# An expert's pass that holds 96 token rows in place of 128, in a decoder step with a mixture of experts

## The reference, cut to what matters

```python
logits = h @ w_router + b_router              # (288, 8)
top_p, top_e = top_k(softmax(logits), 2)      # two experts of eight for each token
top_p = top_p / sum(top_p)
# assignments sorted by expert, each expert sees only its own tokens
y_e = (silu(x_e @ w_gate[e]) * (x_e @ w_up[e])) @ w_down[e]   # 1024 -> 3584 -> 1024
out[token] += top_p * y_e[slot of the token]
```

## Time and profile before

| | |
|---|---|
| median of three runs | 1741.95 us |
| profiled execution: its own time | 1747.82 us |
| its span | 1746.0 us |
| PE busy, share of the span | 1704.5 us, 98% |
| DVE, ACT busy | 78%, 60% |
| expert stage on PE (first L2350 at 742.8, last at 1730.5) | about 988 us |

### The profile page before, as it was taken

The page is one execution under the profiler, slowest core; times in us unless marked ns, Lnnn a source line. Parts: engine busy times, 40 slices in busy tenths (PEclk is TensorE's granted clock), DMA queues, the critical chain, the costliest instruction groups (busy, mean ns, idle before and its releaser), DMA issues.

```text
span 1746.0 us, 25370 instructions
## 1 busy us (share of the span) xinstructions
PE 1704.5 (98%) x9394; PEld 1430.4 (82%) x9394; DVE 1364.7 (78%) x1601; ACT 1042.8 (60%) x1006; POOL 98.1 (6%) x118
## 2 busy tenths in 40 slices
PE   6999999999999999799999999999999999999998
PEld 3878978999988698588888888888888888888886
DVE  2799474554459964888898998998988988989998
ACT  3345424443344533467777777777777777777776
POOL 0112110000021130200000000000000000000000
PEclk8999998999999999999999999999999999999999
DMA  9885047444457601589999999999999999999997
GB/s 383 326 315 193 26 176 282 158 162 168 169 197 283 215 25 55 203 327 343 350 378 350 360 363 343 373 354 347 358 355 352 364 351 351 375 345 366 361 367 271
DMA packets 73385, 499.49 MB, mean 286 GB/s; under 512 B 8096, under 2 KB 8224, under 8 KB 15296
## 3 DMA queue, kind: packets, MB, share of 16 engines
q1 hardware_dynamic: 69728, 481.17, 72.8%
q0 software_dynamic: 3552, 16.87, 2.5%
HBM read 485.96 MB, written 12.05 MB: 285 GB/s over the span
## 4 chain that ended last, share of the span: by engine, by line
PE 90%; DVE 7%; DMA 1%; issue 1%; ACT 1%; SPq 0%; DVEq 0%; ACTq 0%
PE ps L2350 17%; PE ps L2352 17%; PE ps L2351 17%; PE ps L1789 5%; PE ps L1791 5%; PE ps L1790 5%; PE ps L2149 4%; PE ps L1978 3%; DVE yc L1193 2%; PE ps L1800 2%; PE ps L2327 1%; DMA raw<-units 1%; PE ps L1886 1%; PE ps L1901 1%; PE ps L1899 1%; PE ps L2294 1%
## 5 line engine op out<-in xcount | busy, mean ns | idle before, releaser
L1117 DVE TENSOR_TENSOR wlo<-raw,whi 128x2048 fp32r<-128x2048 f32 x382 | 872.8, 2293 | 174.5 <-ACT whi L721 173.5
L721 ACT ACTIVATE whi<-raw 128x2048 fp32r<-128x2048 f32 x384 | 736.5, 1918 | 257.9 <-PE ps L2352 206.5
L2350 PE MATMUL ps<-whi,ht_hi 128*128 128x512 f32 x896 | 355.8, 397 | 3.2 <-DVE ht_lo L1679 3.2
L2351 PE MATMUL ps<-wlo,ht_hi 128*128 128x512 f32 x896 | 350.0, 391 | 0.0
L2352 PE MATMUL ps<-whi,ht_lo 128*128 128x512 f32 x896 | 349.9, 391 | 0.0
L2350 PEld LDWEIGHTS ps<-whi,ht_hi 128*128 128x128 f32 x896 | 168.6, 188 | 36.4 <-issue 3.5
L2352 PEld LDWEIGHTS ps<-whi,ht_lo 128*128 128x128 f32 x896 | 168.6, 188 | 36.0
L2351 PEld LDWEIGHTS ps<-wlo,ht_hi 128*128 128x128 f32 x896 | 168.9, 188 | 31.7
L2350 PE MATMUL ps<-whi,at_hi 128*128 128x512 f32 x448 | 175.2, 391 | 0.0
L2352 PE MATMUL ps<-whi,at_lo 128*128 128x512 f32 x448 | 174.4, 389 | 0.0
L2351 PE MATMUL ps<-wlo,at_hi 128*128 128x512 f32 x448 | 174.4, 389 | 0.0
(11 more groups left out here) (357 smaller groups left out, 2003.8 us busy)
## 6 DMA issues: line engine op xcount, KB each, us to landing
raw<-units SPq DMA_DIRECT2D x447, 1024.0 KB, 6.1
raw<-units SPq DMA_DIRECT2D x16, 512.0 KB, 5.8
sst<-gdn_in POOLq DMA_DIRECT2D x8, 512.0 KB, 6.0
gdns_out<-sst POOLq DMA_DIRECT2D x8, 512.0 KB, 4.1
qst_out<-qpad POOLq DMA_DIRECT2D x2, 1890.0 KB, 10.8
cst_out<-cpad POOLq DMA_DIRECT2D x2, 1116.0 KB, 12.9
x<-x_in SPq DMA_DIRECT2D x1, 1152.0 KB, 9.2
y_out<-hf SPq DMA_DIRECT2D x2, 576.0 KB, 2.9
```

The costliest lines, as they stand in the source:

```text
L721: act.activation(whi[s % NSPLIT][:, :], raw[u % NRAW][:, :], ACT.Copy).then_inc(hi_split, 1)
L1117: dve.tensor_tensor(wlo[s % NSPLIT][:, :], raw[unit_of(s) % NRAW][:, :], whi[s % NSPLIT][:, :].bitcast(F32), ALU.subtract).then_inc(lo_spl ...
L2350: mm(ps[:, bank, :], a_hi[:, a], whi[u % NSPLIT][:, w], start=(first and i == 0), stop=False)
L2351: mm(ps[:, bank, :], a_hi[:, a], wlo[u % NSPLIT][:, w], start=False, stop=False)
```

## The change

The constant SLOTS = 96 takes the place of 128 in the experts' part. Stationary operands are 96 columns wide (their storage still steps by 128, so that the columns used of a 512-column tile are four pieces of 96). Results have 96 partitions. The four transposes of a group have an identity of 96x96 as moving operand in place of 128x128, and 96 rows of the stationary one. The rounding and the rest behind a transpose (`at_hi`, `at_lo`, `ht_hi`, `ht_lo`) run on 4x96 columns in place of 512; the others (`sge`, `ae`, `xe`, `ye_hi`, `ye_lo`) keep their columns and lose partitions. The scatter contracts over 96 rows. The passes are counted by 96 and 192 in place of 128 and 256. Sizes and positions of all tiles in memory stay, and so do the weights, their transfers, and the splitting of weights into `whi` and `wlo`.

```diff
+SLOTS = 96
+def slots(rows, half=0):
+    return rows[:, half * 512:(half + 1) * 512].rearrange("p (i n) -> p i n", n=P)[:, :, 0:SLOTS]
...
-                    act.activation(ht_hi[q][:, (part - 2) * 512:(part - 1) * 512], ps[:, bank, :], ACT.Copy).then_inc(hthi_ready, 1)
+                    act.activation(slots(ht_hi[q], part - 2), slots(ps[:, bank, :]), ACT.Copy).then_inc(hthi_ready, 1)
...
-                            act.activation(at_hi[c % 2][:, :], ps[:, 4, :], ACT.Copy).then_inc(eahi_ready, 1)
+                            act.activation(slots(at_hi[c % 2]), slots(ps[:, 4, :]), ACT.Copy).then_inc(eahi_ready, 1)
...
-            step(dve.tensor_scalar(npf2[:, 0:1], npf[:, 0:1], 128.5, 1.0, ALU.is_gt, ALU.add))
-            step(dve.scalar_tensor_tensor(npf[:, 0:1], npf[:, 0:1], 256.5, npf2[:, 0:1], ALU.is_gt, ALU.add))
+            step(dve.tensor_scalar(npf2[:, 0:1], npf[:, 0:1], SLOTS + 0.5, 1.0, ALU.is_gt, ALU.add))
+            step(dve.scalar_tensor_tensor(npf[:, 0:1], npf[:, 0:1], 2 * SLOTS + 0.5, npf2[:, 0:1], ALU.is_gt, ALU.add))
...
-                            dve.tensor_tensor(at_lo[c % 2][:, :], ps[:, 4, :], at_hi[c % 2][:, :].bitcast(F32), ALU.subtract)\
+                            dve.tensor_tensor(slots(at_lo[c % 2]), slots(ps[:, 4, :]), slots(at_hi[c % 2]).bitcast(F32), ALU.subtract)\
...
-                                dve.tensor_tensor(ae[c % 2][:, :], ps[:, 2 + c % 2, :], sge[c % 2][:, :], ALU.mult)\
+                                dve.tensor_tensor(ae[c % 2][0:SLOTS, :], ps[0:SLOTS, 2 + c % 2, :], sge[c % 2][0:SLOTS, :], ALU.mult)\
...
-                        last = pe.transpose(ps[:, bank, d * P:(d + 1) * P], xe[:, c:c + P], cc("ident"))
+                        last = pe.transpose(ps[:, bank, d * P:d * P + SLOTS], xe[0:SLOTS, c:c + P], cc("ident", SLOTS, SLOTS))
...
-                mm(ps[:, bank, 0:T], ye_hi[:, w], pt_sel[q][:, :], start=True, stop=False)
+                mm(ps[:, bank, 0:T], ye_hi[0:SLOTS, w], pt_sel[q][0:SLOTS, :], start=True, stop=False)
...
-                                last = pe.transpose(ps[:, 4, i * P:(i + 1) * P], ae[c % 2][:, i * P:(i + 1) * P], cc("ident"))
+                                last = pe.transpose(ps[:, 4, i * P:i * P + SLOTS], ae[c % 2][0:SLOTS, i * P:(i + 1) * P], cc("ident", SLOTS, SLOTS))
...
-                                a = slice((off + i) * P, (off + i + 1) * P)
+                                a = slice((off + i) * P, (off + i) * P + SLOTS)
                                 w = slice(i * 512, (i + 1) * 512)
-                                mm(ps[:, bank, :], a_hi[:, a], whi[u % NSPLIT][:, w], start=(first and i == 0), stop=False)
-                                mm(ps[:, bank, :], a_hi[:, a], wlo[u % NSPLIT][:, w], start=False, stop=False)
-                                last = mm(ps[:, bank, :], a_lo[:, a], whi[u % NSPLIT][:, w], start=False, stop=(end and i == 3))
+                                mm(ps[0:SLOTS, bank, :], a_hi[:, a], whi[u % NSPLIT][:, w], start=(first and i == 0), stop=False)
+                                mm(ps[0:SLOTS, bank, :], a_hi[:, a], wlo[u % NSPLIT][:, w], start=False, stop=False)
+                                last = mm(ps[0:SLOTS, bank, :], a_lo[:, a], whi[u % NSPLIT][:, w], start=False, stop=(end and i == 3))
```

More of the change, by code:

```diff
@@ L1065, in gather @@
                     act.wait_ge(gx_done, g * 2 + part + 1)
-                    act.activation(xe[:, part * 512:(part + 1) * 512], ps[:, bank, :], ACT.Copy).then_inc(gx_copied, 1)
+                    act.activation(xe[0:SLOTS, part * 512:(part + 1) * 512], ps[0:SLOTS, bank, :], ACT.Copy).then_inc(gx_copied, 1)
                 elif part < 4:
                     act.wait_ge(gt_done, g * 2 + part - 1)
-                    act.activation(ht_hi[q][:, (part - 2) * 512:(part - 1) * 512], ps[:, bank, :], ACT.Copy).then_inc(hthi_ready, 1)
+                    act.activation(slots(ht_hi[q], part - 2), slots(ps[:, bank, :]), ACT.Copy).then_inc(hthi_ready, 1)
             def output_high(it, q, a):
@@ L1074, in output_high @@
                 act.wait_ge(unit_used, later(S_MOE + PER_EXPERT - 1 + a, it, PER_EXPERT))
-                act.activation(ye_hi[:, a * 512:(a + 1) * 512], ps[:, 5 + a, :], ACT.Copy, scale=pslot[q])\
+                act.activation(ye_hi[0:SLOTS, a * 512:(a + 1) * 512], ps[0:SLOTS, 5 + a, :], ACT.Copy, scale=pslot[q][0:SLOTS])\
                     .then_inc(yhi_ready, 1)
@@ L1098, in _ @@
                                     act.wait_ge(eg_prod, it * FC + c - 1)
-                                act.activation(sge[c % 2][:, :], ps[:, c % 2, :], ACT.Silu).then_inc(eg_gate, 1)
+                                act.activation(sge[c % 2][0:SLOTS, :], ps[0:SLOTS, c % 2, :], ACT.Silu).then_inc(eg_gate, 1)
                                 if c:
@@ L1676, in gather @@
                 if 2 <= part < 4:
-                    cols = slice((part - 2) * 512, (part - 1) * 512)
                     dve.wait_ge(hthi_ready, g * 2 + part - 1)
-                    dve.tensor_tensor(ht_lo[q][:, cols], ps[:, bank, :], ht_hi[q][:, cols].bitcast(F32), ALU.subtract)\
+                    dve.tensor_tensor(slots(ht_lo[q], part - 2), slots(ps[:, bank, :]), slots(ht_hi[q], part - 2).bitcast(F32), ALU.subtract)\
                         .then_inc(htlo_ready, 1)
@@ L1698, in output_low @@
                 dve.wait_ge(yhi_ready, it * 2 + a + 1)
-                dve.scalar_tensor_tensor(ye_lo[:, a * 512:(a + 1) * 512], ps[:, 5 + a, :], pslot[q],
-                                         ye_hi[:, a * 512:(a + 1) * 512].bitcast(F32),
+                dve.scalar_tensor_tensor(ye_lo[0:SLOTS, a * 512:(a + 1) * 512], ps[0:SLOTS, 5 + a, :], pslot[q][0:SLOTS],
+                                         ye_hi[0:SLOTS, a * 512:(a + 1) * 512].bitcast(F32),
                                          ALU.mult, ALU.subtract).then_inc(ylo_ready, 1)
             def next_pass(p_):
-                dve.tensor_scalar(posm, posm, -128.0, None, ALU.add)
-                dve.tensor_scalar(posT[0:NE, :], posT[0:NE, :], -128.0, None, ALU.add).then_inc(pass_step, 1)
+                dve.tensor_scalar(posm, posm, -float(SLOTS), None, ALU.add)
+                dve.tensor_scalar(posT[0:NE, :], posT[0:NE, :], -float(SLOTS), None, ALU.add).then_inc(pass_step, 1)
                 dve.wait_ge(pass_step, p_ + 1)
@@ L2293, in gather @@
                             pe.wait_ge(tok_lo_ready, i - 1)
-                        last = mm(ps[:, bank, :], pe_sel[:, b * P:(b + 1) * P],
+                        last = mm(ps[0:SLOTS, bank, :], pe_sel[:, b * P:b * P + SLOTS],
                                   tok[:, b * D + part * 512:b * D + (part + 1) * 512], start=(i == 0), stop=(i == 4))
@@ L2311, in scatter @@
                 w = slice(d * P, (d + 1) * P)
-                mm(ps[:, bank, 0:T], ye_hi[:, w], pt_sel[q][:, :], start=True, stop=False)
-                mm(ps[:, bank, 0:T], ye_lo[:, w], pt_sel[q][:, :], start=False, stop=True).then_inc(scat_done, 1)
+                mm(ps[:, bank, 0:T], ye_hi[0:SLOTS, w], pt_sel[q][0:SLOTS, :], start=True, stop=False)
+                mm(ps[:, bank, 0:T], ye_lo[0:SLOTS, w], pt_sel[q][0:SLOTS, :], start=False, stop=True).then_inc(scat_done, 1)
             with pe.Fori(0, n_pass) as p_:
```

## The result

The changed kernel takes 1751.62 us (median of 20 runs, 1744.42 to 1756.56), the one before 1747.31 us (median of 20 runs taken beside them, 1741.62 to 1751.66). The ratio is 1.0027, interval 1.0015 to 1.0038: some 4.7 us slower (4.3 by the medians). I had forecast 1734.5, within 1720 to 1744, and 7.5 us of gain. The first three runs of before lay low by this measure (1741.95); with 1747.31 in its place the forecast would have been 1739.8. So of the 17.1 us between forecast and result 5.4 come from the reference point, and 11.8 from what I said of the change.

What follows compares the result with a forecast made beforehand. PE's matmul steps were taken to bound the experts' stage. Transposes -7.2 us and the first expert's wait -0.3, expert matmuls 0, made -7.5 from 1741.95: 1734.5 us, range 1720 to 1744.

Steps and rivals of the forecast that it cites:

- What bounds the kernel: Experts' stage: PE, never idle, sets the pace by number of matmuls times step; DMA at most 0.97, nothing late next.
- The transposes: 288 transposes on PE's path, 128 to 96 moving columns: 0.112 to 0.084-0.088 us each, 7.2 us saved.
- Rival 1: Transposes do not get shorter, as a fixed cost or the 128-column load paces them; 1741.7 us, chance 0.18.
- The expert matmuls: 4032 matmuls keep 512 moving columns; the shorter stationary load is already hidden, so their change is 0.
- surcharge: About 0.013 us of each 0.226 us expert matmul step, on top of 0.2133 us for 512 columns at 2.4 GHz.
- rival 3: Expert matmuls: a 96-column load no longer hides behind the matmul before; fully exposed 80 ns each, 2057 us, chance 0.07.
- the 4 ns: Exposed load time per expert matmul beyond which the kernel would be over 0.5% slower.
- Rival 2: Expert matmuls: surcharge shrinks with the stationary columns, 13 us less, 1721 us; wholly gone 52 less, 1682; chance 0.13.
- The half clock: Expert matmuls at granted clock 0.50 step 0.4275 us against 0.4267, no surcharge; taken as evidence for 0 change.
- ACT, DVE, passes, transfers: Shorter roundings save DVE about 9.7 us that PE does not wait for; one pass and 336 units stay.
- The 0.3 us ahead of the first expert: PE's 3.2 us wait for `ht_lo` shortens, as two DVE instructions lose 0.13 us each.

Runs made afterwards that it cites:

- part 6: 64 or 128 bytes left free ahead of `whi` and `wlo`, in the short-transposes kernel (1756.5, 1764.53 us) and the changed kernel (1761.45, 1758.0 us).

## Why the prediction was wrong

**What bounds the kernel** was right: PE without idle time, DMA at 0.94 to 0.97, waits as foretold.

**The transposes: right in kind and in the price of one.** Three steps inside each group fell from 109.0 to 83.3 ns (I said 0.084 to 0.088 us), 5.4 us, with the short transposes alone as in the whole change. The term of the sum was 7.2. The first matmul behind a group gives another 1.8 in the whole change, but not with the transposes alone (314 ns against 314.6 before), so that the total of 7.2 is partly luck. The rule of the Trainium skill that I held against it ("TensorE: Matmul & The Clock Gate", PE-mode transpose: its time lies mostly in the access to memory) had no effect on the pace: the record of one still lasts 245 ns, and a new one starts every 83.3. Rival 1 is out. Taken alone the edit brought 4.4 us by the timed runs, interval 1.7 to 7.2.

**The expert matmuls: the step that failed.** "0.109 is far below 0.226, so a load of 96 columns makes shorter something that is hidden already. I take 0 for these 4032." The load is hidden, but the step is not the stream's time alone: 13 ns of surcharge stand in it, and I priced only what a shorter load could take away from them, or what an exposed load would add. Measured: +3.2 ns on a settled step, +9.8 us over the stage once the gain behind the transposes is taken out, +8.8 us by the runs of the matmuls alone, where I had 0. That is the mild form of rival 3 (0.23, as the prediction's last part said it would look), but not by its mechanism: the load became shorter (188 to 162 ns) and nothing was exposed. It stayed under the 4 ns at which I had it decide, since I measured that from a gain of 7.5 us. I gave the rival 0.07 and read its bound as "over 0.5% slower", so the mild form had no chance of its own and my range ended at 1744. (The 0.25 us that I took off to get 0.109 stands in no row that I showed; the trace has 0.253 us for one of these matmuls.)

Rival 2 had the wrong sign. The Trainium skill (same page, Back-to-back issue gap) says that load and matmul together set the spacing; as I read it, a shorter load can only help, and 127 to 64 columns here show 229.0 to 233.4 ns against 226.8 with loads down to 135 ns. The half clock, which I used as evidence for 0, showed only that the surcharge is absent there at either width (0.427 us before and after); it says nothing on what full clock does with it.

**What is shown and what is argued.** Shown: in this kernel, at full clock, the surcharge of a matmul with 512 columns is 13 to 20 ns, fixed by the program, and changed by the width of the stationary block, by its place, and by the place of the moving tile, none in a steady direction. The pairs of part 6 show that what counts of the places is how PE's two operands stand against each other. Not every shift changes it: `whi` begins 53376 bytes into a partition, the experts' tiles from 139904 on, 128 more than a multiple of 512, and only the `at_hi` and `at_lo` of odd chunks begin 256 bytes off that grid (at 172416 and 174464). Their settled steps in the kernel before are 226.7 ns on the mean of 300, those of the even chunks 226.7 on 520. So a distance of 256 bytes costs nothing, while 64 and 128 do. With 128 columns in blocks every 512 bytes all matmuls keep one relation up to such 256 bytes. Fewer columns move the end of the block, and blocks at 384 bytes, a shift or a gap of 64 or 128 bytes move the whole of it against the stream; each gave a longer step.

Argued, and not shown: that the load of the next block and the moving stream are read beside each other and meet in memory. ACT's and DVE's writes into `whi` and `wlo` are not needed for the account, since the pairs have one cycle with these writes in different places. The Trainium skill ("SBUF — State Buffer", Terms) gives PE and ACT ports of their own, which speaks against ACT's writes too. Why one distance is good and another bad stays open.

**ACT, DVE, passes, transfers** cost nothing, as predicted; PE waited for none of them longer than before. The 0.3 us ahead of the first expert, the other term of the sum, came out as 0.1 (3.2 to 3.1).

## What to carry to other kernels

Where PE sets the pace as here, edit the moving operand for time and leave the stationary one alone: fewer moving columns shortened each step (transposes 109 to 83 ns), fewer stationary ones shortened only a load that was hidden. The stream of matmuls carried a surcharge that depends on where its operands stand, so after any edit of widths, tile sizes or placement measure the settled step, the distance over some forty starts, and not only the busy time. When it has grown with no wait in sight, shift one operand by some tens of bytes before you look for a cause in the work. Such a shift is a test, and not a cure that can be counted on: of those tried here, none made the experts' step shorter than before.

## What the runs showed of the hardware that I had not expected

- Three settled means recur: 226.8, 230.0 and 233.3 ns, at 2.4 GHz 544, 552 and 560 cycles, 8 apart. The last stands with 120 columns, with 80 (233.4), with 96 and a gap of 64 bytes, and at three steps in four with 127. Other means stand between them (228.8 to 229.4, 231.1 to 232.6), so it is no rule.
- A shift can shorten a step too. In the first layer the weights are the stationary operand, 288 columns move, and 526 steps follow each other in one row. Without the gap (the kernel with short transposes) and with 64 bytes:

```profile
420.20 0.30 PE L1796 MATMUL ps<-act_lo,whi 128*128 128x288 f32 x1
...
490.32 0.29 PE L1797 MATMUL ps<-act_hi,wlo 128*128 128x288 f32 x1
```

```profile
422.08 0.29 PE L1797 MATMUL ps<-act_lo,whi 128*128 128x288 f32 x1
...
491.63 0.29 PE L1798 MATMUL ps<-act_hi,wlo 128*128 128x288 f32 x1
```

  70.12/526 = 133.3 ns against 69.55/526 = 132.2 ns. It is 133.3 also in the kernel before, in the changed one and with 128 bytes, and 132.2 in both kernels with 64. The same 64 bytes cost the experts 2.0 ns a step and give this layer 1.1.
- A transpose of 96 rows keeps a load of 140 ns and goes at 83 ns all the same. From 128 to 96 moving columns its pace went from 109.0 to 83.3 ns, 0.8 ns a column, where a column of the expert matmuls takes 0.44. No kernel here cuts the moving columns without the rows, so the two are not told apart.
